# The first mixer of a two-block kernel by pairs of heads: split scores, mask as a product, decay rows by DMA

## The reference, cut to what matters

```python
h = rms_norm(x, norm_mix_g); z = h @ w_in       # 1024 -> 2 x 512 + 3 x 512 + 8
u_a, v_a = gelu(...), gelu(...)                  # 8 heads of 64 each
# spatial gating, per block of 128 tokens and per head
vn = layer_norm(v_a) * ln_g
mixed = einsum('hts,bnshd->bnthd', where(mask, w_s, 0), vn) + b_s
out_a = u_a * mixed
# forgetting attention, 8 heads of 64, blocks of 128 queries
c = cumsum(log_sigmoid(f_logit))
s = q @ k.T / 8 + c[query] - c[key]              # keys after the query: -inf
out_b = softmax(s) @ v
x = x + concat([out_a, out_b]) @ w_out
```

## Time and profile before

| | us |
|---|---|
| median of 3 runs | 1058.18 (1056.96 to 1058.52) |
| profiled execution, own time | 1061.31 |
| its span, first to last instruction | 1059.6 |
| TensorE busy in the span | 1012.8 (96%), weight loads 802.1 |
| VectorE / ScalarE / GpSimd busy | 636.5 / 296.7 / 72.6 |
| mean granted clock of TensorE | 0.981 of full speed |

### The profile page before, as it was taken

The page is one execution under the profiler, slowest core; times in us unless marked ns, Lnnn a source line. Parts: engine busy times, 40 slices in busy tenths (PEclk is TensorE's granted clock), DMA queues, the critical chain, the costliest instruction groups (busy, mean ns, idle before and its releaser), DMA issues.

```text
span 1059.6 us, 14008 instructions
## 1 busy us (share of the span) xinstructions
PE 1012.8 (96%) x4854; PEld 802.1 (76%) x4854; DVE 636.5 (60%) x1128; ACT 296.7 (28%) x534; POOL 72.6 (7%) x140
## 2 busy tenths in 40 slices
PE   5999999799999999999999998999999889999998
PEld 4876655478888888888888887788888767787877
DVE  5245775726677677777433344777678788534443
ACT  4132343513232222222011025533222234403210
POOL 1010000000111001111101101000000000000000
PEclk9999999799999999999999999899999979999999
DMA  8754222036555666555565545344333200023444
GB/s 293 252 186 131 82 80 90 30 121 196 177 193 189 195 198 198 196 189 186 182 198 193 179 145 198 120 161 157 123 116 119 80 1 1 2 82 105 133 147 171
DMA packets 44944, 153.52 MB, mean 145 GB/s; under 512 B 4960, under 2 KB 5728, under 8 KB 44896
## 3 DMA queue, kind: packets, MB, share of 16 engines
q1 hardware_dynamic: 21888, 75.51, 21.7%
q0 software_dynamic: 19584, 71.31, 20.7%
q10 hardware_dynamic: 3424, 6.04, 1.7%
HBM read 148.64 MB, written 4.19 MB: 144 GB/s over the span
## 4 chain that ended last, share of the span: by engine, by line
PE 78%; DVE 11%; DMA 4%; ACT 4%; issue 3%; POOLq 0%; ACTq 0%; DVEq 0%
PE bank L499 63%; DMA HI<-wstream 4%; PE bank L638 2%; PE bank L619 1%; PE bank L552 1%; DVE LO L1339 1%; DVE QNR L1726 1%; PE bank L799 1%; PE bank L558 1%; PE bank L868 1%; PE bank L887 1%; DVE YM L1632 1%; PE bank L858 1%; PE bank L838 1%; PE bank L628 1%
## 5 line engine op out<-in xcount | busy, mean ns | idle before, releaser
L499 PE MATMUL bank<-GH,HI 128*128 128x512 f32 x720 | 293.3, 407 | 2.4 <-ACT DV L1187 1.0
L499 PE MATMUL bank<-GL,HI 128*128 128x512 f32 x720 | 282.6, 392 | 0.0
L499 PE MATMUL bank<-GH,LO 128*128 128x512 f32 x720 | 282.5, 392 | 0.0
L1339 DVE TENSOR_TENSOR LO<-RAW,HI 128x1024 fp32r<-128x1024 f32 x92 | 112.4, 1222 | 173.9 <-DMA HI<-wstream 172.4
L499 PEld LDWEIGHTS bank<-GH,HI 128*128 128x128 f32 x720 | 136.5, 190 | 37.4 <-issue 6.9
L499 PEld LDWEIGHTS bank<-GH,LO 128*128 128x128 f32 x720 | 136.2, 189 | 29.8
L499 PEld LDWEIGHTS bank<-GL,HI 128*128 128x128 f32 x720 | 136.5, 190 | 24.6
L487 POOL DMA_DIRECT2D HI<-wstream x132 | 70.1, 531 | 962.0 <-PE bank L499 952.1
L1097 ACT ACTIVATE YC<-AB,PAR 128x512 f32<-128x512 f32 x44 | 36.0, 818 | 140.7 <-DVE AB L1490 140.7
L499 PE MATMUL bank<-AH,LO 128*128 128x512 f32 x176 | 70.2, 399 | 0.0
L499 PE MATMUL bank<-AL,HI 128*128 128x512 f32 x176 | 69.4, 394 | 0.0
(11 more groups left out here) (274 smaller groups left out, 1428.0 us busy)
## 6 DMA issues: line engine op xcount, KB each, us to landing
RAW<-wstream SPq DMA_DIRECT2D x136, 512.0 KB, 3.6
HI<-wstream POOLq DMA_DIRECT2D x136, 512.0 KB, 5.0
X<-x_t SPq DMA_DIRECT2D x8, 256.0 KB, 13.2
out_t<-X ACTq DMA_DIRECT2D x8, 256.0 KB, 2.1
XR<-out_t ACTq DMA_DIRECT2D x8, 256.0 KB, 2.6
out_t<-XR SPq DMA_DIRECT2D x8, 256.0 KB, 3.1
CON<-consts ACTq DMA_DIRECT2D x1, 704.0 KB, 5.9
SGW<-sgw_t ACTq DMA_DIRECT2D x1, 512.0 KB, 8.4
```

The source lines that it names most:

```text
L499: mm = pe.matmul(out, a, b, start=(first and n == 0), stop=(last and n == 2))
L1339: dve.tensor_tensor(LO[:, u % RING, :], RAW[:, u % RING, :], HI[:, u % RING, :].bitcast(F32), ALU.subtract).then_inc(unit_split, 1)
```

## The change

All in the first mixer. The list now has 18 slots, one for each block of 128 queries of a *pair* of heads (16 slots, and two to finish).

- **Scores** (`A`, L659). Queries and keys are split like the activations: ScalarE makes the high part after the evacuation, VectorE the rest (new entry `lowqk`, L1481). A visit is six fp32r matmuls, two heads on the two halves of the rows in turn, and the causal mask is added by two products of an identity with a mask tile (L662). Each head of the pair has one bank, so a visit waits for the exponentials of the one before.
- **Decay rows.** No `K`. ScalarE stores the eight rows of -c to a part of the output tensor in HBM (16 KB), waits, and loads them back spread over all partitions (2 MB). VectorE's maximum (L1459) is one instruction over the whole width with this bias.
- **Normalising** (`N`). VectorE makes two reciprocals at once (L1490); ScalarE scales the weights (two copies with a scale).
- **Weighted values** (`C`, L683): the two heads of a pair alternate, for the two halves of the bank's partitions. They are split straight from the bank (L1504).
- **Gates** all use bank 7 and stand in slots 8 to 11, beside the last two units of products.
- **Output product.** `product_mixed` now makes three output tiles (banks 0, 1, 7) and stands in slots 12 to 16; a fourth tile (`later`) is begun before the last attention tile is split; the rest follows. The weight units are laid out to match. The layer norm's first stages stand ahead of the first visit.

```diff
...
+def _pairs():
+
+    slots = []
+    for n in range(18):
+        slot = [("A", n)] if n < 16 else []
+        if n >= 5 and n % 4 == 1:
+            slot += [("C", n // 4 - 1), ("split", n // 4 + 3)]
+        if 1 <= n <= 16:
+            slot.append(("B", n - 1))
+        if n < 16:
+            slot.append(("N", n))
+        slots.append(slot)
+    return slots
...
-    return (products(0, 2) + [("K", 0)] + products(2, 3)[:2] + part(0, 8, products(2, 6)[2:])
-            + part(8, 16, _merge(products(6, 9), [("ln", (n, b)) for n in range(3) for b in range(NB)]))
-            + part(16, 24, products(9, 11)) + part(24, 27, products(11, 12) + [("gelu", 0)])
-            + part(27, 30, [("gate", p) for p in range(4)])
-            + part(30, 33, [("split", k) for k in range(7)] + [("wo", 0), ("wo", 1)])
-            + part(33, 35, [("wo", k) for k in range(2, 6)]) + [("split", 7), ("wo", 6), ("wo", 7)])
+        out = []
+        for n in range(a, b):
+            what, m = MIX1_UNITS[n]
+            out += [(what, (m, 0))] + ([("lowqk", MIX1_UNITS[n - 1][1])] if n and MIX1_UNITS[n - 1][0] == "qk" else [])
+            out += [(what, (m, q)) for q in range(1, 4)]
+        return out
...
+    norms = [("ln", x) for x in ((0, 0), (0, 1), (1, 0), (0, 2), (1, 1), (0, 3), (1, 2), (1, 3))]
+    first = products(0, 3)
+    return (_merge(first[:11], norms) + part(0, 4, _merge(first[11:] + products(3, 6), [("ln", (2, b)) for b in range(NB)]))
+            + part(4, 8, products(6, 10))
+            + part(8, 12, products(10, 12) + [("lowqk", 7), ("gelu", 0)] + [("gate", p) for p in range(4)])
+            + part(12, 16, [("split", k) for k in range(4)] + [("wo", k) for k in range(5)])
+            + part(16, 17, [("wo", 5)]) + [("wo", 6)] + slots[17][:1] + [("later", 0)] + slots[17][1:] + [("wo", 7)])
...
                 if k == 0:
                     pe.wait_ge(gated, 4)
-                    pe.wait_ge(exp_made, 32)
-                u = U_WO + k // 2
-                pe.wait_ge(unit_split, u + 1)
-                pe.wait_ge(ml_made, k + 1)
-                for m in range(4):
-                    mm = three(PS[m][:, :], ring(u, 4 * (k % 2) + m), (MH[:, k, :], ML[:, k, :]), k,
+                    pe.wait_ge(gemm_freed, G_WO)
+                mixed_made(k)
+                for m in range(3):
+                    n = 3 * k + m
+                    u = U_WO + n // 8
+                    if n % 8 == 0:
+                        pe.wait_ge(unit_split, u + 1)
+                    mm = three(mixed_bank(m)[:, :], ring(u, n % 8), (MH[:, k, :], ML[:, k, :]), k,
                                k == 0, k == KC - 1)
...
+                p, i = n // 4, n % 4
+                w = P * (i + 1)
...
-                    pe.wait_ge(gemm_freed, G_QK + turn_of("qk", 2 * (h // 2) + 1) + 1)
+                    pe.wait_ge(qk_split, 2 * p + 2)
...
+                for part, (q, k) in enumerate(((MH, KH), (MH, KL), (ML, KH))):
+                    for e in range(2):
+                        if n and part == 0:
+                            pe.wait_ge(exp_made, 2 * n + e - 1)
+                        r = slice(64 * e, 64 * e + 64)
+                        pe.matmul(PS[2 + e][:, 0:w], q[r, 4 + p, P * i:P * (i + 1)], k[r, p, 0:w],
+                                  start=(part == 0), stop=False)
+                for e in range(2):
+                    pe.matmul(PS[2 + e][:, P * i:w], IDF[:, :], CSF[:, :], start=False, stop=True).then_inc(s_made, 1)
...
-                    mm = pe.matmul(PS[6][r:r + 64, P * j:T], VB[:, j, 64 * h:64 * (h + 1)], PT1[:, j, P * j:T],
-                                   start=(j == 0), stop=(j == NB - 1))
+                    for e in range(2):
+                        mm = pe.matmul(PS[6][64 * e:64 * e + 64, P * j:T], VB[:, j, P * p + 64 * e:P * p + 64 * (e + 1)],
+                                       PT1[:, e, j, P * j:T], start=(j == 0), stop=(j == NB - 1))
...
-                pe.wait_ge(gemm_freed, G_WO)
-                if p >= 2:
-                    pe.wait_ge(gated, p - 1)
+                if p:
+                    pe.wait_ge(gated, p)
+                else:
+                    pe.wait_ge(va_freed, 4)
...
+            act.wait_ge(negc_ready, 1)
+            act.dma_start(out_t[0:8, :], FR[0:8, 2, :]).then_inc(negc_stored, 16)
...
+            act.wait_ge(negc_stored, 16)
+            act.dma_start(NCB[:, :, :], out_t[0:8, :].unsqueeze(0).to_broadcast([P, 8, T])).then_inc(ncb_landed, 16)
...
+                elif what == "qk" and n[1] == 3:
+                    m = n[0]
+                    act.wait_ge(gemm_freed, G_QK + turn_of("qk", m) + 1)
+                    act.activation(MH[:, 4 + m // 2, :] if m % 2 == 0 else KH[:, m // 2, :],
+                                   MT[:, 4 + m // 2, :] if m % 2 == 0 else KT1[:, m // 2, :], ACT.Copy)\
+                       .then_inc(qk_high, 1)
...
+                        c = (2 * n + e) % 16
+                        act.wait_ge(max_made, 2 * n + e + 1)
...
+                            act.wait_ge(pt_mm, 2 * n + e - 3)
+                        act.activation(P1[:, 2 * (n % 2) + e, 0:w], PS[2 + e][:, 0:w], ACT.Exp, scale=-1.0,
+                                       bias=MX1[:, c:c + 1], accum_out=SU1[:, c:c + 1]).then_inc(exp_made, 1)
+                elif what == "N":
+                    w = P * (n % 4 + 1)
+                    act.wait_ge(rc_made, n + 1)
+                    for e in range(2):
+                        c = (2 * n + e) % 16
+                        p = P1[:, 2 * (n % 2) + e, 0:w]
+                        act.wait_ge(exp_made, 2 * n + e + 1)
+                        act.activation(p, p, ACT.Copy, scale=RC1[:, c:c + 1]).then_inc(p_ready, 1)
...
+                    act.wait_ge(gated, n + 1)
+                    act.activation(MH[:, n, :], MT[:, n, :], ACT.Copy).then_inc(mg_high, 1)
...
+                    act.wait_ge(pv_made, n - 3)
+                    act.activation(MH[:, n, :], PS[6][:, :], ACT.Copy).then_inc(ma_high, 1)
...
+            def biased_max(n, e):
+
+                w = P * (n % 4 + 1)
+                c = (2 * n + e) % 16
+                S = PS[2 + e][:, 0:w]
+                dve.wait_ge(ncb_landed, 16)
+                dve.wait_ge(s_made, 2 * n + e + 1)
+                dve.tensor_tensor_reduce(S, S, NCB[:, 2 * (n // 4) + e, 0:w], -1.0, 3e38, ALU.add, ALU.min,
+                                         MX1[:, c:c + 1]).then_inc(max_made, 1)
...
+                elif what == "lowqk":
+                    t = n // 2
+                    rest, full, top = ((ML[:, 4 + t, :], MT[:, 4 + t, :], MH[:, 4 + t, :]),
+                                       (KL[:, t, :], KT1[:, t, :], KH[:, t, :]))[n % 2]
+                    dve.wait_ge(qk_high, n + 1)
+                    dve.tensor_tensor(rest, full, top.bitcast(F32), ALU.subtract).then_inc(qk_split, 1)
...
+                    c = 2 * n % 16
+                    dve.wait_ge(exp_made, 2 * n + 2)
+                    dve.reciprocal(RC1[:, c:c + 2], SU1[:, c:c + 2]).then_inc(rc_made, 1)
...
+                    dve.wait_ge(ma_high, n - 3)
+                    dve.tensor_tensor(ML[:, n, :], PS[6][:, :], MH[:, n, :].bitcast(F32), ALU.subtract)\
+                       .then_inc(ma_made, 1)
...
```

More of the change, by code:

```diff
@@ L209, in _ring @@
         out.append((what, n))
-        if what in ("qk", "u") and n[1] == 1:
+        if what in ("qk", "u") and n[1] == 3:
             out.append(("ring", U_QK + MIX1_UNITS.index((what, n[0])) + RING - 1))
@@ L213, in _ring @@
             out.append(("ring", U_WO + RING - 1))
-        elif what == "wo" and n in (3, 5):
-            out.append(("ring", U_WO + RING + n // 4))
+        elif what == "wo" and n == 4:
+            out.append(("ring", U_WO + RING))
         elif what == "ba":
@@ L242 @@
 )
-PCOL = [P * i * (i + 1) // 2 for i in range(NB)]
-PALL = P * NB * (NB + 1) // 2
 def build(nc, x_t, wstream, params, consts, sgw_t, sgb, out_t):
@@ L616, in scores @@
+                if n == 0:
                     pe.wait_ge(vb_freed, 4)
[L617 to L630 removed]
@@ new lines, in scores @@
+                for e in range(2):
+                    pe.matmul(PS[2 + e][:, P * i:w], IDF[:, :], CSF[:, :], start=False, stop=True).then_inc(s_made, 1)
+            def turn(n):
+                i = n % 4
+                for e in range(2):
+                    pe.wait_ge(p_ready, 2 * n + e + 1)
+                    if n >= 1:
+                        pe.wait_ge(pt_freed, 2 * n + e - 1)
+                    else:
+                        pe.wait_ge(vb_freed, 4)
+                    for j in range(i + 1):
+                        mm = pe.transpose(PS[4 + e][:, P * j:P * (j + 1)],
+                                          P1[:, 2 * (n % 2) + e, P * j:P * (j + 1)], IDENT)
+                    mm.then_inc(pt_mm, 1)
@@ L664, in _ @@
                     turn(n)
+                elif what == "later":
+                    pe.wait_ge(exp_made, 32)
+                    product_later(3, range(KC - 1))
```

228 lines of the change are left out of this document (93 added, 135 removed).

## The result

The changed kernel takes 1043.2 us (median of 4 runs, 1039.78 to 1044.74); the kernel before, beside it, 1058.35 (1056.96 to 1060.95). The ratio is 0.9839, 95% interval 0.9815 to 0.9863: 15.1 us saved where 11.8 were forecast. A later set gave 0.9843 (0.9827 to 0.9859). The profiled execution is the fastest of the four, own time 1039.78 and span 1038.1, while the one of before (1061.31) was slower than all four beside it. So the profiled pair differs by 21.5 us, more than the medians do.

What follows compares the result with a forecast made beforehand. TensorE was taken as the bound to 175 us, then attention's chain of waits. 23.0 us less work plus 12.8 of old stalls minus 24.0 of new ones gave 11.8 off 1058.2: 1046.4 us, range 1032 to 1057.

Steps and rivals of the forecast that it cites:

- Scores, 29.2 to 19.8: TensorE's score work in the first mixer: 29.2 us before, sixteen visits at 1.24 us, 19.8 in all, after.
- equal visits at all widths: Sign that the forecast is right: score visits near 1.24 us, whatever the number of keys.
- D: Rival, chance 0.06: fp32r halves run one after the other, visits 1.50, weighted values 4.6 a pair; 1058 us, no change.
- The six matmuls of a visit: Six fp32r score matmuls on 64 rows, taken as bound by six weight loads, 0.66 us a visit.
- Weighted values, 18.4 to 10.0: TensorE's weighted values: heads alternating between column halves take 2.5 us a pair, ends 2.3 and 2.7.
- Decay rows, 5.2 us and hidden: One-row products worth 5.2 us leave TensorE; the 2 MB load replacing them lands at 88 to 90 us, hidden.
- Old stalls, 12.8: TensorE's idle time and lower clock between 175 and 214 us in the old kernel, 12.8 us, all go.
- First scores, 9.0 + 2.7: TensorE waits 9.0 us for the split of k's first tile on VectorE, then loses 2.7 at the lower clock.
- Gates and tail, 9.3 + 3.0: Serial gate loops on one bank and late slots 12 and 13: 9.3 us idle, 3.0 for the clock.
- rival A: Chance 0.22: visits at 0.83, no lower clock in the tail, gate chain half hidden; 12.5 us less, 1034.
- B: Rival, chance 0.08: the mixer becomes a chain over VectorE and ScalarE, decay rows landing at 98; 1059 us, no change.
- C: Rival, chance 0.08: fp32r matmuls on 64 rows hide no weight load, visits 3.0 us, 28 more in all; 1075.

Runs made afterwards that it cites:

- e12: The changed kernel unedited, measured again in a later set beside other runs; 1042.13 us, ratio 0.9843 to the kernel before.
- e7: The changed kernel without the two causal-mask products of each score visit; 1037.06 us, ratio 0.9773.
- e4: The changed kernel with a pair's weighted values issued one head after the other instead of alternating; 1049.98 us, ratio 0.9897.
- e6: The changed kernel with layer norm behind the first scores, gelu and gates earlier, q's copy and k's split moved ahead; 1029.84 us, ratio 0.9704.
- e1: The changed kernel with the layer norm's first stages moved from ahead of the first scores to later slots; 1036.34 us, ratio 0.9774.
- e3: The changed kernel with gelu and gates moved earlier, between the last products; 1034.89 us, ratio 0.9773.
- e9: e6 with the decay rows in two transfers and the gates alternating between two banks; 1027.30 us, ratio 0.9696.

## Why the prediction was right, and where its terms were off

The direction and the places were right: 11.8 us forecast, 15.1 measured. The profiled pair shows 20.2 us at the mixer's end (0.4 of it a start earlier), and with e12 as the changed kernel it would be 16.5. Term by term, from the first profile:

- **Scores, 29.2 to 19.8.** Mis-sized, the largest error of work. The step taken was six weight loads at 0.11 us each, "1.24 us a visit at any width". Measured: 0.90 to 1.31 with the keys, mean 1.08, 17.3 us. The test named for this, equal visits at all widths, failed. The growing widths are not D's either, since the halves did overlap.
- **The six matmuls of a visit.** They take 0.48, 0.55, 0.72 and 0.89 us. From 256 keys on the middle pair steps as long as one matmul of its width (0.12, 0.18 and 0.24 us), so no load shows; at 128 keys it steps 0.11, what one further transpose costs, not two and not the 0.06 of its columns. The mean of the six, 0.66, is the figure that I took, by luck: the mechanism was wrong, and too much at narrow visits made up for too little at wide ones. The masks were right (0.22, e7). What was mis-sized on the mean is the switch, 0.36 in the sum for 0.18 in and 0.18 back, and about 0.2 measured in all: 0.16 x 16 = 2.5 us. A switch of the masks' own does not show either (e7). The upper end of the range has a slip: six matmuls at 0.231 us per 512 columns are 0.87 us on the mean, not 0.92. The Trainium skill ("TensorE: Matmul & The Clock Gate", LDWEIGHTS) gives 107 ns a load, an estimated 0.64 us for six in a row; six loads and six matmuls of 128 columns took 0.48 us here, so loads one after another do not bound this sequence.
- **Weighted values, 18.4 to 10.0.** 9.2 at full clock (2.30 a pair between starts); the lower bound was the right row, and e4 shows why.
- **Decay rows, 5.2 us and hidden.** Right. 9.1 us to land, between the bounds, with 2 us to spare; e6 shows that they are the next to be late. The 5.2 us are counted from rows; no kernel here puts the old products back.
- **Old stalls, 12.8.** All gone, and with them 2.5 of the 2.72 us of small waits that I had left in both kernels.
- **First scores, 9.0 + 2.7.** 8.44 idle, k's split at 84.94 + 0.68 = 85.6 against 86.6, about 2.2 for the clock (18 products 5.63 us instead of 4.1, the visit some 0.6 more). e1 shows the cause.
- **Gates and tail, 9.3 + 3.0.** 6.87 idle: the loops were 2.75 us, as reckoned, then 3.64 at the low clock. The 2.5 us of slots 12 and 13 did not show, because TensorE got there late at half speed. e3 brings them back. The clock cost more, about 4.3: two gates 1.76, the weighted values 0.94, eight transposes 0.89 (1.93 against 1.04), two visits some 0.8. Together 11.2 against 12.3: near by luck, since less idle time and a dearer clock make up for each other, and in e12 the same waits cost some 2.4 us more at the low clock.

So of the 8 us by which the profiled mixer beat the sum, 3.3 are work, 2.5 small waits and 2.2 stalls; how much of it is the luck of that execution e12 puts at up to 3.8. Of rival A's three parts the visits came 2.5 of 6.5 us its way; the gates were not half hidden (6.87 us idle, where I had 6.8 for them), and the clock did fall, twice. B's wait for the rows came only from e6 on, where the other gap was gone; C and D did not happen.

## What to carry to other kernels

Issue two half-array matmuls alternately: on column halves the second was then free and in turn it was not (e4); on row halves alternate pairs cost one head's step too, but no other order was tried. Whether the scores are fp32 or split fp32r hardly matters. Look at what stands on every in-order queue between a producer and the first consumer: work moved "out of the way" ahead of it cost 7 us here, and moving it back into covered slots was worth as much as half of the whole change. A hole of some microseconds is paid twice, once idle and again at half clock (behind every hole of 2.6 to 7.7 us ahead of the first scores, but not behind those of 1.07 in e6 and 1.54 in e9), and one that is closed uncovers the next. Here the gains stopped when the next wait was set by a transfer.
